# Dealing the spare slot tiles of a mixture-of-experts stage out to the experts in a fixed order, in a one-core hybrid attention / DeltaNet / MoE step

## The chip, the cores and the metric

One core of a Trainium2 chip runs the whole kernel. The metric is the device time of one execution in microseconds, lower is better. An execution is also profiled once, and its trace shows the span from its first instruction to its last.

## The reference, cut to what matters

The kernel computes one layer of a trunk for 256 context and 1024 latent tokens (1280 in all, model width 1024): a mixer (softmax attention beside a gated DeltaNet), then a hierarchical mixture of experts, then a final RMS norm. All of it is float32. The change touches the mixture of experts alone:

```python
g_top, g_idx = lax.top_k(gp, 1)                    # 1 of 4 groups
e_top, e_idx = lax.top_k(ep, TOP_K_IN_GROUP)       # 2 of the 4 experts in it
expert = g_idx * EXPERTS_PER_GROUP + e_idx         # 16 experts
hid = jax.nn.silu(einsum('td,edf->tef', t, w_gate)) * einsum('td,edf->tef', t, w_up)
hid = hid * combine[..., None]                     # 0 for the experts not chosen
y = einsum('tef,efd->td', hid, w_down)             # w_gate, w_up 1024x256, w_down 256x1024
```

## The kernel before

The kernel goes through seven stages, with a meeting of all five engines ("arrivals") between them. The sixth ends with the router and the expert tiles, the seventh combines.

**Slots and tiles.** Each token has two entries, one for each expert chosen: 2560 entries. They are sorted by expert into tiles of 128 slots, and a tile holds entries of one expert only. An expert with c entries needs ceil(c/128) tiles, and at least one is given to it. The number of tiles is fixed when the kernel is built, since no loop has a length read from data: MT = 2560/128 + 16 - 1 = 35, the most that any routing can need. For these inputs the reference's router gives the 16 experts 141, 53, 349, 403, 88, 66, 71, 107, 183, 152, 87, 164, 310, 136, 132 and 118 entries, which is 2, 1, 3, 4, 1, 1, 1, 1, 2, 2, 1, 2, 3, 2, 2 and 1 tiles, 29 together. Six tiles are spare.

**The table (VectorE, L1845 to L1899).** After the router's counts have been summed over the tokens on TensorE (L1062, L1064), VectorE works out `r_nt`, the tiles of each expert (L1846 to L1850), then `r_base`, the tiles of the experts ahead (L1853, L1855), then the running ends `r_nt + r_base` (L1857). Every one of these is a small instruction that waits for the one ahead of it. From the base it works out each entry's slot (L1859 to L1865) and one-hot matrices, with which TensorE (L1069) writes down the token of each slot. From the ends it counts for each tile the experts that have ended (L1882 to L1892): that is the tile's expert, held down to the last one by a minimum (L1886). The spare tiles lie behind all ends, so they run with expert 15 (weights of the ring slot that it is in); an empty slot holds token 0, and nobody reads what a spare tile puts out.

```python
v.tensor_scalar(r_nt, r_nt, 1.0, None, ALU.max)           # L1850
v.tensor_tensor(earlier, precedes, bc(r_nt...), ALU.mult) # L1853
v.tensor_reduce(r_base, earlier, AX.X, ALU.add)           # L1855
v.tensor_tensor(r_nt, r_nt, r_base, ALU.add)              # L1857
```

**The weights (SyncE's DMA queue, L632 to L657).** An expert's weights are 3 MB in three transfers (gate and up at L637, down at L639). They live in a ring of three places. The first three experts are loaded ahead of the stage. After that SyncE goes through the experts in order; `dn_mm` counts two halves of a down product for each tile:

```python
for e in range(NE):
    sp.wait_ge(S[f"ew_in{e % RING_E}"], landed(e, RING_E, 3))   # L652 expert e has landed
    sp.sem_inc(S["ew_ready"], 1)                                # L653 TensorE may use expert e
    if 1 <= e and e + RING_E - 1 < NE:
        through = sp.value_load(tab_i[... e - 1 ...])           # L655 2 x tiles up to expert e-1
        sp.wait_ge(S["dn_mm"], through)                         # L656
        expert_load(e + RING_E - 1)                             # L657 into the place of expert e-1
```

**The tiles (TensorE, L1099 to L1114).** In turn t TensorE does the gate and up products of tile t (16 matmuls, L1084), turns the hidden rows of tile t-1 (L1109), turns the slots of tile t+1 (L1079) and does the down product of tile t-1 (8 matmuls, L1094). Ahead of the gate and up products it waits until `ew_ready` has reached the tile's expert, plus one (L1103). GpSimd gathers the rows of each tile (L2060, an indirect DMA), ScalarE empties PSUM (L1370, L1389, L1379) and stores each tile (L1381), VectorE does the hidden product (L1906, L1908) and a copy (L1916).

**The last stage** gathers each token's two rows from the stored tiles by `pos_i` (GpSimd, L2071), combines, norms and stores them.

The small constants are one table of 485 columns, loaded once at the start, from which `small_row` takes rows (L137 to L140). `R`, the large buffer that holds the ring of weights and nearly all other tiles, is allocated behind it in SBUF.

Of the kernel before, what the change touches and what calls it, by code (L numbers as in the profile page):

```python
# [18 lines left out]
ALU = mybir.AluOpType  # L19
ACT = mybir.ActivationFunctionType  # L20
AX = mybir.AxisListType

P = 128
# [13 lines left out]
NE, FF = 16, 256  # L37
SLOTS = 128
MT = HT = 2 * T // SLOTS + NE - 1
# [33 lines left out]
def small_constants():  # L73

    step = [e % RING_E for e in range(NE)]
    rows = [np.arange(T // SLOTS) * float(SLOTS), np.arange(HT), (np.arange(NE)[None, :] < np.arange(NE)[:, None]).ravel(),
            [6144.0 * (step[e + 1] - step[e]) if e + 1 < NE else 0.0 for e in range(NE)], 128.0 * np.arange(MT + 1), np.arange(P) - 128.0, [4, 3, 2, 1]]
    row = np.concatenate([np.asarray(r, np.float32) for r in rows])
    return np.broadcast_to(row, (P, row.size)).copy()

# [11 lines left out]
def build(nc, a, outs):  # L92
    ctx = ExitStack()
    with ctx:
# [3 lines left out]
        def sem(name):  # L98
            return ctx.enter_context(nc.semaphore(name))


        const_np, small_np = shape_constants(), small_constants()
        cos_np, sin_np = rotary_tables()
        const_d = nc.inline_tensor(const_np, name="shape_constants")
# [29 lines left out]
        def small_row(n):  # L134
            sat[0] += n
            return small[:, sat[0] - n:sat[0]]

        filled, unit_no = small_row(T // SLOTS), small_row(HT)
        precedes = small_row(NE * NE).rearrange("p (e f) -> p e f", e=NE)
        slot_step, k128, lane, first4 = small_row(NE), small_row(MT + 1), small_row(P), small_row(4)  # L140


        prm = sb("prm", [P, P])
# [51 lines left out]
        S = {n: sem(n) for n in names}  # L195
# [3 lines left out]
        def count(name):  # L199


            counts[name] += 1
            return counts[name]
# [212 lines left out]
        def rsc(*shape):  # L416
            n = int(np.prod(shape))
            rat[0] += n
            r = R3[:, rat[0] - n:rat[0]]
            if len(shape) == 2:  # L420
                r = r.rearrange("p (a b) -> p a b", a=shape[0])
            return r
# [8 lines left out]
        r_cmp = rsc(HT * NE)  # L431
        r_nt, r_base = rsc(NE), rsc(NE)
# [235 lines left out]
        def _(pe):  # L668
# [179 lines left out]
            def values(i):  # L848
                _, nk, v0 = keys(QH[i][0])
                end = TURN0[i, 1] + len(slices(i))  # L850
                pe.wait_ge(S["pt_act"], emptied(end, "act"))
                if emptied(end, "dve") > 0:
                    pe.wait_ge(S["pt_dve"], emptied(end, "dve"))
                if i > 0:
                    pe.wait_ge(S["o_out"], i)
                for j in range(nk):
                    for g in range(2):
                        lo = slice(g * HD, (g + 1) * HD)
                        last = mm(ps[lo, 7, (i % 4) * P:(i % 4 + 1) * P], v_sb[:, v0 + j, lo], pT[i % 2][g][:, j, :],
                                  start=(j == 0), stop=(j == nk - 1))  # L860
                last.then_inc(S["pv_mm"], 1)
# [551 lines left out]
        def _(dve):  # L1413
            v = nc.vector

            def bc(x, shape):
                return x.to_broadcast([P] + shape)
# [431 lines left out]
            dve.wait_ge(S["dve_chain"], count("dve_chain"))  # L1849
            v.tensor_scalar(r_nt, r_nt, 1.0, None, ALU.max).then_inc(S["dve_chain"], 1)  # L1850
            dve.wait_ge(S["dve_chain"], count("dve_chain"))
            earlier = r_cmp[:, 0:NE * NE].rearrange("p (e k) -> p e k", e=NE)
            v.tensor_tensor(earlier, precedes, bc(r_nt.unsqueeze(1), [NE, NE]), ALU.mult).then_inc(S["dve_chain"], 1)  # L1853
            dve.wait_ge(S["dve_chain"], count("dve_chain"))
# [251 lines left out]
```

## Time and profile before

| | us |
|---|---|
| median of three runs | 2481.5 (2478.1 to 2483.27) |
| time of the profiled execution | 2483.28 |
| its span | 2481.4 |
| TensorE matmul busy | 2155.5 (87%) |
| VectorE / ScalarE / GpSimd busy | 943.3 / 673.1 / 217.0 |
| mean granted TensorE clock | 0.93 |

The profile has one line for each engine and kind of instruction. "Idle before" is time in which the engine stood still just ahead of an instruction, with what ended it. SPq is the queue of DMA issues and semaphore steps of SyncE. Times of a timeline are microseconds from the start of the span. A matmul of 128x512 in float32 goes through TensorE as several passes, and its row is that of the whole matmul.

### The profile page before, as it was taken

What the parts mean: (1) busy time and instruction counts of PE and PEld (TensorE: products, weight loads), DVE (VectorE), ACT (ScalarE), POOL (GpSimd) and SP (SyncE); (2) the same over time, 40 slices, a digit from 0 to 9 for tenths busy, and PEclk for the clock granted to TensorE, in tenths of its full rate; (3) what the DMA queues carried; (4) which work ended last, traced back from release to release, by engine and by line L of the source; (5) the groups of instructions that cost most, each with busy time, mean ns of one, the idle gap of its engine ahead of it and who ended that gap; (6) DMA issues with size and microseconds to landing.
All of it is one profiled execution on the core that took longest, in us unless ns stands there. A gap on an engine that the chain in (4) does not pass through costs nothing. (4 is left out here: it accounts for less than half of the span.)

```text
span 2481.4 us, 39269 instructions
## 1 busy us (share of the span) xinstructions
PE 2155.5 (87%) x16431; PEld 1329.5 (54%) x16431; DVE 943.3 (38%) x1820; ACT 673.1 (27%) x1366; POOL 217.0 (9%) x301
## 2 busy tenths in 40 slices
PE   5987999989998588987897999999998699899960
PEld 4545677665554487887754555555455444344420
DVE  3254666643784367667460011010233200000116
ACT  6122766652441223322230000000111122122223
POOL 2000000000000233232000000000000000000013
PEclk8997999999999799989998999999998699999985
DMA  9423000000100232332103121120413455765226
GB/s 325 142 87 114 11 4 1 2 38 25 36 1 0 44 64 44 64 62 42 55 0 94 27 50 26 26 68 1 146 66 128 137 183 182 259 236 207 85 102 203
DMA packets 256382, 210.09 MB, mean 85 GB/s; under 512 B 147468, under 2 KB 219472, under 8 KB 255568
## 3 DMA queue, kind: packets, MB, share of 16 engines
q1 hardware_dynamic: 242032, 158.16, 21.5%
q0 software_dynamic: 9136, 31.06, 3.9%
q10 hardware_dynamic: 5040, 18.35, 1.8%
q8 instruction: 133, 2.18, 0.4%
q14 instruction: 41, 0.34, 0.0%
HBM read 165.37 MB, written 42.01 MB: 84 GB/s over the span
## 5 line engine op out<-in xcount | busy, mean ns | idle before, releaser
L741 PE MATMUL ps<-R 128*128 128x512 f32 (+1 forms) x816 | 300.2, 529 | 11.3 <-SPq L529 8.4
L1008 PE MATMUL ps<-R 128*128 128x512 f32 (+1 forms) x768 | 286.3, 527 | 19.4 <-DMA R<-in_w_dn_br_dram 17.3
L1084 PE MATMUL ps<-R 128*128 x560 | 260.2, 620 | 25.4 <-SPq L653 22.2
L741 PEld LDWEIGHTS ps<-R 128*128 128x128 f32 x816 | 157.5, 194 | 151.0 <-issue 132.4
L1008 PEld LDWEIGHTS ps<-R 128*128 128x128 f32 x768 | 147.5, 193 | 151.7 <-issue 144.3
L900 PE MATMUL ps<-R 64*64 64x64 f32 x5120 | 179.3, 228 | 55.5 <-DVE R L1674 44.0
L900 PEld LDWEIGHTS ps<-R 64*64 64x64 f32 x5120 | 168.8, 143 | 73.0 <-DVE R L1674 47.3
L1084 PEld LDWEIGHTS ps<-R 128*128 128x128 f32 x560 | 111.0, 200 | 169.2 <-issue 169.2
L1749 DVE TENSOR_TENSOR R<-ps,R 128x512 f32<-128x512 f32 (+1 forms) x48 | 28.9, 602 | 393.9 <-ACT R L1341 393.1
L1916 DVE COPY R<-ps 128x256 f32<-128x256 f32 x35 | 14.9, 424 | 383.4 <-PE ps L1109 383.4
L1523 DVE TENSOR_SCALAR_CACHE_REDUCE R<-ps 128x512 f32<-128x512 f32 (+1 forms) x208 | 128.3, 666 | 60.6 <-PE ps L826 60.5
L1030 PE MATMUL ps<-R 128*128 128x512 f32 x320 | 142.4, 604 | 3.8 <-PEq L1017 3.8
L1010 PE MATMUL ps<-R 128*128 128x512 f32 (+1 forms) x384 | 145.4, 521 | 0.0
L1341 ACT ACTIVATE R<-ps 128x512 f32<-128x512 f32 (+1 forms) x48 | 25.2, 526 | 412.1 <-PE ps L1010 411.4
L2060 POOL DMA_INDIRECT R<-h_scratch,slot_i x35 | 32.9, 941 | 1125.0 <-DVE slot_i L1899 750.2
L1094 PE MATMUL ps<-R 128*128 x280 | 127.8, 599 | 1.5 <-DVE R L1916 1.3
L845 PEld LDWEIGHTS ps<-cst,R 128*128 128x128 f32 x800 | 87.7, 142 | 59.1 <-issue 48.6
L845 PE MATMUL ps<-cst,R 128*128 128x128 f32 x800 | 106.6, 282 | 5.7 <-ACT R L1239 2.9
L826 PE MATMUL ps<-R 64*128 64x512 f32 (+1 forms) x416 | 107.1, 619 | 3.7 <-SPq L513 3.6
L1229 ACT ACTIVATE R<-R 128x1536 f32<-128x1536 f32 (+1 forms) x80 | 108.6, 1357 | 3.0 <-DVE R L1532 2.9
L1010 PEld LDWEIGHTS ps<-R 128*128 128x128 f32 x384 | 73.1, 190 | 64.4 <-issue 61.2
L1030 PEld LDWEIGHTS ps<-R 128*128 128x128 f32 x320 | 61.3, 194 | 78.6 <-issue 73.9
(266 smaller groups left out, 2675.1 us busy)
## 6 DMA issues: line engine op xcount, KB each, us to landing
R<-in_w_mod_dram SPq DMA_DIRECT2D x12, 2048.0 KB, 9.0
slot_output<-R ACTq DMA_DIRECT2D x35, 512.0 KB, 3.5
R<-in_w_gate_e_dram SPq DMA_DIRECT2D x16, 1024.0 KB, 6.3
R<-in_w_up_e_dram SPq DMA_DIRECT2D x16, 1024.0 KB, 10.1
R<-in_w_down_e_dram SPq DMA_DIRECT2D x16, 1024.0 KB, 12.1
R<-in_w_in_dram SPq DMA_DIRECT2D x30, 512.0 KB, 5.4
R<-tu_scratch SPq DMA_DIRECT2D x80, 128.0 KB, 3.2
R<-in_x_sample_dram SPq DMA_DIRECT2D x16, 512.0 KB, 6.1
```

Of the source, the lines that this page charges most:

```text
L741: last = mm(ps[:, u % 4, 0:w], w_sb[n % NW][:, k, :], hT[:, k, c0:c0 + w], start=(k == 0), stop=(k == KD - 1))
L826: last = mm(ps[:, 2 * (u % 2) + g, 0:w], qT[lo, h4, qt * P:(qt + 1) * P], kT[lo, c0 + j * 512:c0 + j * 512 + w], start=True, stop=True)
L845: last = turn128(ps[:, 4 + v % 3, k * P:(k + 1) * P], s_sb[i % 2][g][:, j * 512 + k * P:j * 512 + (k + 1) * P], ident)
L900: last = mm(ps[lo, bank, a * C:(a + 1) * C], lhs(a)[lo], rhs(a)[lo], start=start and (alone or a == 0), stop=stop and (alone or a == PAIRS ...
L1008: mm(ps[:, o + x, 0:w], wk[:, x, k, :], hT[:, k, c0:c0 + w], start=(k == 0), stop=(k == KD - 1))
L1010: last = mm(ps[:, o + 2 + x, 0:w], wb[:, x, k, :], (aoT, odT)[x][:, k, c0:c0 + w], start=(k == 0), stop=(k == 3))
L1030: last = mm(ps[:, 2 * (n % 2) + h, :], mT[:, k, n * P:(n + 1) * P], ow[k][:, h * 512:(h + 1) * 512], start=(k == 0), stop=(k == KD - 1))
L1084: last = mm(ps[:, 2 + t % 2, :], hsT[t % 2][:, k, :], R[:, bass.ds(at + (RB + k * 512), 512)], start=(k == 0), stop=(k == KD - 1))
L1094: last = mm(ps[:, 5 + u % 3, :], hidT[t % 2][:, k, :], R[:, bass.ds(at + (RB + 4096 + k * D + h * 512), 512)], start=(k == 0), stop=(k == 1))
L1229: f(s_sb[i % 2][g][:, 0:w], s_sb[i % 2][g][:, 0:w], ACT.Exp, bias=shift[i % 2][g], accum_out=sums[qt % 2][:, g, h4:h4 + 1]).then_inc(S["p_ ...
L1523: v.tensor_scalar(s_sb[i % 2][g][:, j * 512:j * 512 + w], ps[:, 2 * (u % 2) + g, 0:w], HD ** -0.5, None, ALU.mult, ALU.max, accum_out=tops ...
L2060: pool.indirect_dma_start(hs[t % 2], None, h2_d, bass.IndirectOffsetOnAxis(ap=slot_i[:, t:t + 1], axis=0)).then_inc(S[f"hs_in{t % 2}"], 16)
```

## The change

Three small VectorE instructions are put between L1850 and L1853. They sum the tiles over the experts, compare "sum + place of the expert in the order" with 35, and give one more tile to each expert for which that is smaller. The place is the expert's number with its four bits reversed: 0, 8, 4, 12, 2, 10, 6, 14, 1, 9, 5, 13, 3, 11, 7, 15 is the order in which experts are served. These 16 numbers are a new row at the end of the small constants (501 columns in place of 485). Everything that is worked out from `r_nt` (bases, slots, each tile's expert, the counts on which the loads of weights wait) follows by itself. The number of tiles stays 35.

```diff
-            [... 128.0 * np.arange(MT + 1), np.arange(P) - 128.0, [4, 3, 2, 1]]
+            [... 128.0 * np.arange(MT + 1), np.arange(P) - 128.0, [4, 3, 2, 1],
+            [int(f"{e:04b}"[::-1], 2) for e in range(NE)]]
...
-        slot_step, k128, lane, first4 = small_row(NE), small_row(MT + 1), small_row(P), small_row(4)
+        slot_step, k128, lane, first4, turn_of = small_row(NE), small_row(MT + 1), small_row(P), small_row(4), small_row(NE)
...
             v.tensor_scalar(r_nt, r_nt, 1.0, None, ALU.max).then_inc(S["dve_chain"], 1)
             dve.wait_ge(S["dve_chain"], count("dve_chain"))
+            v.tensor_reduce(r_base[:, 0:1], r_nt, AX.X, ALU.add).then_inc(S["dve_chain"], 1)
+            dve.wait_ge(S["dve_chain"], count("dve_chain"))
+            v.tensor_scalar(r_cmp[:, 0:NE], turn_of, r_base[:, 0:1], float(MT), ALU.add, ALU.is_lt).then_inc(S["dve_chain"], 1)
+            dve.wait_ge(S["dve_chain"], count("dve_chain"))
+            v.tensor_tensor(r_nt, r_nt, r_cmp[:, 0:NE], ALU.add).then_inc(S["dve_chain"], 1)
+            dve.wait_ge(S["dve_chain"], count("dve_chain"))
             earlier = r_cmp[:, 0:NE * NE].rearrange("p (e k) -> p e k", e=NE)
```

## Rows read from the trace of the kernel before

**Rows 1.** The page: the span, and the chain that ended last, by engine

```profile
span 2481.4 us, 39269 instructions
...
PE 41%; DVE 2%; DMA 2%; SPq 1%; issue 1%; ACT 1%; POOL 0%; DVEq 0%; ACTq 0%; PEldq 0%; POOLq 0%
```

**Rows 2.** Waits of TensorE, 1940 to 2405 us: total us, times, longest

```profile
PE ps L1084 <- SPq L653: 22.2, 6, 5.9
PE ps L1079 <- DMA R<-h_scratch,slot_i: 5.6, 1, 5.6
```

**Rows 3.** Timeline of TensorE: start, us, line, count, [idle before <- releaser]

```profile
1981.21 7.03 PE L1084 MATMUL ps<-R 128*128 x16
...
1996.34 8.83 PE L1084 MATMUL ps<-R 128*128 x16 [3.51 <-SPq L653]
...
2086.18 3.64 PE L1094 MATMUL ps<-R 128*128 x8
2093.26 9.88 PE L1084 MATMUL ps<-R 128*128 x16 [3.43 <-SPq L653]
...
2113.59 9.96 PE L1084 MATMUL ps<-R 128*128 x16 [5.88 <-SPq L653]
...
2131.09 7.13 PE L1084 MATMUL ps<-R 128*128 x16 [2.97 <-SPq L653]
...
2146.02 8.83 PE L1084 MATMUL ps<-R 128*128 x16 [3.22 <-SPq L653]
...
2208.41 8.63 PE L1084 MATMUL ps<-R 128*128 x16 [3.23 <-SPq L653]
...
2244.68 7.03 PE L1084 MATMUL ps<-R 128*128 x16
...
2381.96 7.03 PE L1084 MATMUL ps<-R 128*128 x16
```

**Rows 4.** Timeline of SyncE's DMA issues, same columns

```profile
2089.86 0.37 SPq L637 DMA_DIRECT2D R<-in_w_gate_e_dram  x1
2090.26 0.58 SPq L637 DMA_DIRECT2D R<-in_w_up_e_dram  x1
2090.89 2.16 SPq L639 DMA_DIRECT2D R<-in_w_down_e_dram  x1
...
2108.78 4.61 SPq L639 DMA_DIRECT2D R<-in_w_down_e_dram  x1
2128.15 0.37 SPq L637 DMA_DIRECT2D R<-in_w_gate_e_dram  x1
...
2279.20 0.37 SPq L637 DMA_DIRECT2D R<-in_w_gate_e_dram  x1
```

**Rows 5.** Waits of SyncE's queue, 1700 to 2400 us: total us, times, longest

```profile
SPq L637 <- PE ps L1094: 280.3, 13, 43.5
```

**Rows 6.** Issues that read the down weights: time from issue to landing

```profile
DMA to landing us min/median/max: 11.4/12.1/13.8
```

**Rows 7.** Timeline of VectorE between the router's sums and the table

```profile
1929.25 0.32 DVE L1848 TENSOR_REDUCE R<-R 128x16 f32<-128x160 f32 x1
1929.61 0.17 DVE L1850 TENSOR_SCALAR R<-R 128x16 f32<-128x16 f32 x1
1929.81 0.42 DVE L1853 TENSOR_TENSOR R<-small,R 128x256 f32<-128x256 f32 x1
...
1930.73 0.17 DVE L1857 TENSOR_TENSOR R<-R 128x16 f32<-128x16 f32 x1
1930.93 0.18 DVE L1859 TENSOR_SCALAR R<-R 128x16 f32<-128x16 f32 x1
```

**Rows 8.** Windows: us, PE, PEld, DVE, ACT, POOL busy, PEclk, DMA share, GB/s

```profile
2094.00:2104.00 10.00, 10.00 (x26) 4.70 (x24) 0.55 (x2) 0.55 (x2) 0.00 (x0) 0.76 0.83 303
...
2155.00:2193.00 38.00, 38.00 (x118) 19.06 (x117) 4.71 (x12) 10.37 (x19) 3.74 (x4) 1.00 0.69 233
```

**Rows 9.** The row gathers of the tiles (L2060): time from issue to landing

```profile
DMA to landing us min/median/max: 4.0/4.4/7.6
```

More of the change, by code:

```diff
@@ L76, in small_constants @@
     rows = [np.arange(T // SLOTS) * float(SLOTS), np.arange(HT), (np.arange(NE)[None, :] < np.arange(NE)[:, None]).ravel(),
-            [6144.0 * (step[e + 1] - step[e]) if e + 1 < NE else 0.0 for e in range(NE)], 128.0 * np.arange(MT + 1), np.arange(P) - 128.0, [4, 3, 2, 1]]
+            [6144.0 * (step[e + 1] - step[e]) if e + 1 < NE else 0.0 for e in range(NE)], 128.0 * np.arange(MT + 1), np.arange(P) - 128.0, [4, 3, 2, 1],
+            [int(f"{e:04b}"[::-1], 2) for e in range(NE)]]
     row = np.concatenate([np.asarray(r, np.float32) for r in rows])
```

## The prediction

> **What bounds the kernel now.** I went from the page's chain of waits to the stage that the change touches. The chain is made of TensorE above all [rows 1], so time is won only where TensorE stands still or runs slowly. In the expert stage (1940 to 2405 us) the table of waits shows one costly wait: the gate and up products (L1084) stood still for SyncE's step at L653 six times, 22.2 us together; the other row is the start of the stage [rows 2]. The timeline shows which tiles these were. L1084 has one row per tile; counted from tile 0 they are tiles 3, 11, 12, 13, 14 and 19 [rows 3]. Against the tile counts 2, 1, 3, 4, 1, 1, 1, 1, 2, 2, 1, 2, ... these are the first tiles of experts 2, 5, 6, 7, 8 and 11: each follows an expert with one tile (1, 4, 5, 6, 7 and 10), and no other tile does. Expert 15 has one tile too, but nothing follows it.
>
> The code says why. The release of expert e+1 (L653) stands in SyncE's order behind the load of expert e+2, and that load waits for the last down product of expert e-1. TensorE does that product in the turn after, behind the first gate and up products of expert e. If expert e has one tile, the next thing that TensorE wants is expert e+1. So it ends the down product (2086.18 + 3.64 = 2089.82), only then does SyncE issue three transfers (2089.86 to 2093.05), and at 2093.26 TensorE goes on [rows 3, 4]. Expert e+1 itself has long been in SBUF: it is the issuing that is waited for. If expert e has two tiles or more, the issuing (3 us) lies beside 7.03 us of gate and up products.
>
> The tiles otherwise run at a fixed pace: from 2244.68 (tile 22) to 2381.96 (tile 34) are 12 turns of 11.44 us. From tile 2 (1981.21) to tile 34 are 400.75 us for 32 turns, so 400.75 - 32 x 11.44 = 34.7 us is lost in the stage [rows 3]. The parts: 22.2 us of idle time; slower gate and up products right after it, against 7.03 us: 1.80 + 2.85 + 2.93 + 0.10 + 1.80 + 1.60 = 11.1 us; and 1.4 us of small gaps (0.23 us a stop).
>
> **The change, part by part.** The sum of tiles is 29, so the experts with a place below 6 get one: 0, 8, 4, 12, 2 and 10. The counts become 3, 1, 4, 4, 2, 1, 1, 1, 3, 2, 2, 2, 4, 2, 2, 1, together 35. Experts 4 and 10 have lost their single tile; 1, 5, 6, 7 keep it.
>
> *Stops removed.* Those behind experts 4 and 10: 3.43 + 2.85 + 0.23 = 6.5 us and 3.23 + 1.60 + 0.23 = 5.1 us [rows 3], 11.6 us in all.
>
> *Stops kept.* Four, ahead of tiles 4, 15, 16 and 17. Before, they cost what the rows of tiles 3, 12, 13 and 14 show: 34.7 - 11.6 = 23.1 us. One is larger than the others: 5.88 us, because the issue of one transfer took 4.61 us, against 2.16 us for the same line one expert earlier [rows 3, 4]. I see nothing in the routing that causes it and count it as chance; then a stop is the mean of the other five: idle (3.51 + 3.43 + 2.97 + 3.22 + 3.23)/5 = 3.27, slow products (1.80 + 2.85 + 0.10 + 1.80 + 1.60)/5 = 1.63, gap 0.23, so 5.1 us, and four are 20.5 us. The stage's loss goes from 34.7 to 20.5: 14.2 us won. Bounds: if all four are like the cheapest row (2.97 + 0.10 + 0.23 = 3.3 us), 21.5 us are won; if the first is as tile 3's (5.5) and the other three like the dearest (5.88 + 2.93 + 0.23 = 9.0 us), 34.7 - 32.6 = 2.1 us.
>
> *The clock.* Windows behind a stop show a granted clock of 0.76 and windows of steady work 1.00: part of the stretch ran at 1.2 GHz, in place of 2.4 [rows 8]. Five of the six stops were followed by slower products, one (2.97 us idle) was not [rows 3]. The Trainium skill, TensorE: Matmul & The Clock Gate, Part 1, has it that "the default state is throttled, and activity releases the throttle". If by that rule every stop kept is paid with a slow stretch (the mean of the five is 2.2 us), the four cost 4 x (3.27 + 2.2 + 0.23) = 22.8 us and 11.9 us are won, in place of 14.2. I take the mean over all rows, as one in six got away, and keep the other value inside the range.
>
> *Instructions added.* Three of VectorE, on 16 columns or fewer. They lie on the path: router sums, table, L1069, slot numbers, first gather, first tile; TensorE waits for that gather [rows 2]. The nearest rows, on 128x16, start 0.20 us apart (L1850 to L1853, L1857 to L1859) [rows 7], so three cost 0.6 us. A scalar operand read from SBUF at this size has no row: at most it is like the reduction over 160 columns, 0.36 us from start to start, and then three cost 1.1 us; since each waits for the one ahead, it cannot be below 3 x 0.17 = 0.5 us. Sum row: 0.6 us lost.
>
> *Loads moved.* 13 loads of 3 MB wait on the new counts [rows 5]. A load is released at the last down product of expert e-1 and used by expert e+2: between lie all tiles of experts e and e+1, at least two. Landing takes some 12.1 us (at most 13.8) after its last transfer's issue, which is 1.0 us after the first [rows 4, 6], so about 15 us. The tightest place is two single experts in a row: from the load of expert 8 (2128.15) to its first tile (2146.02) are 18 us [rows 3, 4], 3 us to spare. Experts 5, 6 and 7 keep that pattern unchanged, so nothing new is late. The last load moves behind tile 29 (issued at 2279.20 before, about 2334 after) and is wanted at tile 34, about 2368. The 13 loads cover more of the stage instead of ending ahead of it; what they run beside is the gather of each tile (4.4 us, at most 7.6) [rows 9], which the code issues two turns ahead of its use, and the store of each tile, waited for two turns later. Cost nothing; without that cover, the excess over the slack.
>
> *Spare tiles moved.* Six tiles run earlier with another expert's weights: the same 35 gathers, products and stores, no cost. The last stage gathers the same rows from other places: nothing.
>
> *The table of constants.* 64 bytes more for each of 128 partitions, once, with the other constants at the start: nothing by bytes (8 KB). It moves `R` by 64 bytes, see the third rival.
>
> **The sum.** 14.2 - 0.6 = 13.6 us won. The profiled execution took 2483.3 us (span 2481.4), so it would take 2469.7; it lies 1.8 us above the median of the runs, by which the same gain gives 2467.9. I say 2469, between the two. A measurement of this kernel can tell about 0.2% (5 us) from no change.
>
> **Rivals.**
> 1. *The kept stops become dearer.* For: a 5.88 us stop exists in the before run, at the load of expert 7, which is again in the run of single experts; if it belongs to that load (its addresses or place), it stays, with its slow products: 5.88 - 3.27 = 2.6 and 2.93 - 1.63 = 1.3, so 3.9 us less won, 2473. If more than one stop is like it, 2.1 - 0.6 = 1.5 us are won and the time is 2480: no measurable change. Against: 12 of the 13 later loads were issued without such a delay. Chance: 0.2 for the first form, 0.08 for the second.
> 2. *The stops move instead of going.* If the stops came from late weights, and not from the issuing order, dealing tiles out would shift them to other experts: before minus nothing, plus 0.6 us, 2482. For: the releaser named is the step after a landing wait. Against: TensorE goes on 0.2 us after the last issue in both stops whose issues are shown (2093.05 to 2093.26, 2113.39 to 2113.59) [rows 3, 4], and each stop follows a single-tile expert. The same time would come out if the stage did not get the spare tiles as I count them. Chance 0.05.
> 3. *Slower: the 64 bytes.* `R` goes from a start that is a multiple of 128 bytes to one that is a multiple of 64 only, under all transfers. To end over 5 us slower, 13.6 + 5 = 19 us have to be lost where DMA is exposed. The chain holds 2% of DMA [rows 1], 50 us, so those transfers would have to become some 38% longer. No row shows that alignment matters; nearly all else is hidden. Chance 0.03, time 2487. The Trainium skill, DMA: Bandwidth & Descriptors, "How a descriptor splits into AXI transactions", says that a read that starts off a 256-byte boundary also fetches the bytes from the boundary on. By it a 4 KB row read out of `R` would fetch 192 bytes too much in place of 128, an estimate of 1.5% on stores that are hidden; no row here shows it.
>
> **How the numbers follow.** Four stops near the mean: 0.64, at 2469. Rival 1: 0.28, at 2473 or 2480. Rival 2: 0.05 at 2482. Rival 3: 0.03 at 2487. The forecast's own bounds are 21.5 - 0.6 = 20.9 us won, 2461 from the median, and on the other side rival 1's first form plus half of the spread between the three runs (2.6 us), 2476. That range leaves out the second form of rival 1, rivals 2 and 3, about 0.16. Faster by over 0.2% (below 2476.5): the forecast and the first form, 0.84. Within 0.2%: the second form and rival 2, 0.12. Slower 0.04.
>
> **What would show it.** TensorE's wait for L653: four times, about 13 us together, ahead of tiles 4, 15, 16 and 17, none elsewhere. Steady turns still 11.44 us. From tile 2 to tile 34 about 386.6 us, in place of 400.75. Loads of experts 7, 8 and 9 issued one turn apart, plus the stop, and the last load about 2334. Three VectorE rows of about 0.17 us ahead of the 128x256 product, and the first gather 0.6 us later relative to the router's sums. Everything outside the stage the same within 1 us. I am wrong if the stops number more than four, if a stop is ended by a landing, if the turns with a load beside them are longer than 11.44 us, or if stages ahead of the router change.

## The result and the profile after

The changed kernel takes 2464.56 us (median of four runs, 2463.08 to 2467.85) beside 2479.8 us of the kernel before (four runs): ratio 0.9939, 95% interval 0.9922 to 0.9956. Measured again later (number 8 below) it was 2466.39 beside 2476.84 us: ratio 0.996, 0.9945 to 0.9975. The two intervals share 0.9945 to 0.9956, about 11 to 14 us. The profiled execution took 2467.85 us. Two executions, one of run 1 (2747.1 us) and one of the kernel before beside runs 5 to 7 (3011.29 us), had a granted clock of 0.81 and 0.73 in place of 0.93 and are left out of the ratios, which also need not be exactly the quotients of the medians.

The wait table of TensorE, 1940 to 2405 us, stands against [rows 2] (the added lines of code move L1084 to L1086, L1094 to L1096, and in SyncE's queue L653 to L655, L637 to L639 and L639 to L641):

```profile
PE ps L1086 <- SPq L655: 12.6, 4, 3.6
```

Six stops have become four, and 22.2 us of waiting 12.6. The timeline of TensorE in the changed kernel, against [rows 3] (start, us, line, count, [idle before <- releaser]); the first row is tile 2, the last tile 34:

```profile
1978.73 7.03 PE L1086 MATMUL ps<-R 128*128 x16
...
2004.55 10.19 PE L1086 MATMUL ps<-R 128*128 x16 [2.76 <-SPq L655]
...
2137.32 8.66 PE L1086 MATMUL ps<-R 128*128 x16 [3.62 <-SPq L655]
...
2153.57 8.82 PE L1086 MATMUL ps<-R 128*128 x16 [3.01 <-SPq L655]
...
2170.17 8.83 PE L1086 MATMUL ps<-R 128*128 x16 [3.20 <-SPq L655]
...
2366.44 7.03 PE L1086 MATMUL ps<-R 128*128 x16
```

Counted from tile 0 the stops are ahead of tiles 4, 15, 16 and 17. From tile 2 to tile 34 are 387.71 us, 21.6 us above 32 turns of 11.44 us; before it was 400.75 and 34.7. The stage has won 13.0 us. The span is 15.5 us shorter, though: 2.5 us lie ahead of tile 2 (1981.21 to 1978.73), and behind tile 34 nothing changed (2481.4 - 2381.96 = 99.4 us, 2465.9 - 2366.44 = 99.5 us).

The three new instructions in VectorE's timeline, with the rows around them, against [rows 7]:

```profile
1926.73 0.18 DVE L1852 TENSOR_SCALAR R<-R 128x16 f32<-128x16 f32 x1
1926.94 0.17 DVE L1854 TENSOR_REDUCE R<-R 128x1 f32<-128x16 f32 x1
1927.14 0.24 DVE L1856 TENSOR_SCALAR R<-small,R 128x16 f32<-128x16 f32 x1
1927.42 0.18 DVE L1858 TENSOR_TENSOR R<-R 128x16 f32<-128x16 f32 x1
1927.63 0.43 DVE L1861 TENSOR_TENSOR R<-small,R 128x256 f32<-128x256 f32 x1
```

They take 1927.63 - 1926.94 = 0.69 us. L1856, which reads a scalar from SBUF and does two operations, takes 0.24 us; L1852, with one operation and a constant, 0.18. Which of the two differences costs the 0.06 us isn't shown. SyncE's queue, against [rows 4]: the down weights of experts 5 and 7.

```profile
2066.16 4.40 SPq L641 DMA_DIRECT2D R<-in_w_down_e_dram  x1
...
2134.77 2.34 SPq L641 DMA_DIRECT2D R<-in_w_down_e_dram  x1
```

The long issue is now that of expert 5's down weights (4.40 us) and no longer that of expert 7's (4.61 before, 2.34 now). It lies under expert 3's tiles, where TensorE does not wait for it. The last load is issued from 2332.31 on.

### The profile page after: what moved, and what is told of

Same layout as the page of the kernel before. It is cut to its first block and busy times, and to the rows that moved or that the text cites. A ratio compares the mean times of both kernels' runs of the same rounds, so it can differ in the third digit from the quotient of the medians.

```text
span 2465.9 us, 39272 instructions
## 1 busy us (share of the span) xinstructions
PE 2146.9 (87%) x16431; PEld 1324.6 (54%) x16431; DVE 943.7 (38%) x1823; ACT 673.5 (27%) x1366; POOL 216.9 (9%) x301
## 5 line engine op out<-in xcount | busy, mean ns | idle before, releaser
L1086 PE MATMUL ps<-R 128*128 x560 | 257.2, 614 | 15.8 <-SPq L655 12.6
L1086 PEld LDWEIGHTS ps<-R 128*128 128x128 f32 x560 | 109.8, 197 | 157.4 <-issue 157.4
L1924 DVE COPY R<-ps 128x256 f32<-128x256 f32 x35 | 14.9, 425 | 370.2 <-PE ps L1111 370.2
L1096 PE MATMUL ps<-R 128*128 x280 | 127.7, 599 | 1.3 <-DVE R L1924 1.3
```

Of the source, the lines that this page charges most:

```text
L1086: last = mm(ps[:, 2 + t % 2, :], hsT[t % 2][:, k, :], R[:, bass.ds(at + (RB + k * 512), 512)], start=(k == 0), stop=(k == KD - 1))
L1096: last = mm(ps[:, 5 + u % 3, :], hidT[t % 2][:, k, :], R[:, bass.ds(at + (RB + 4096 + k * D + h * 512), 512)], start=(k == 0), stop=(k == 1))
```

## The experiments

The diffs are cut: the semaphore step behind each VectorE instruction, the names of buffer slices and the middle of long lines (...) are left out.

**1. The layout alone.** The kernel before with 16 unused columns behind the small constants, so that `R` moves by 64 bytes.

```diff
-... np.arange(P) - 128.0, [4, 3, 2, 1]]
+... np.arange(P) - 128.0, [4, 3, 2, 1],
+            np.zeros(NE)]
```

> The kernel before with 16 unused columns added to the small constants: R moves by 64 bytes, nothing else changes. Theory (the gain is stops removed in the expert stage, the rest chance): same time as before within 2.5 us, six stops of TensorE for SyncE's release, 400 us plus or minus 4 from tile 2 to tile 34. Rival A (the move of R is what made the stages ahead of tile 2 some 2.5 us shorter in the changed kernel): 2 to 3 us faster than before, all of it ahead of tile 2. Rival B (the move costs): slower by 2 us or more.

Measured: 2482.07 against 2478.82 us, ratio 1.0007 (0.9996 to 1.0018). Six stops, 397.5 us from tile 2 to tile 34, tile 2 at 1983.4. The move of `R` neither gains nor costs anything that can be seen, and it does not bring tile 2 forward. It leaves no room for a loss above 0.2%.

**2. The instructions without the dealing.**

```diff
-v.tensor_scalar(r_cmp[:, 0:NE], turn_of, r_base[:, 0:1], float(MT), ALU.add, ALU.is_lt)
+v.tensor_scalar(r_cmp[:, 0:NE], turn_of, r_base[:, 0:1], 0.0, ALU.add, ALU.is_lt)
```

> The changed kernel with the threshold 35 made 0, so that the three VectorE instructions run and no expert gets a spare tile. Theory: the gain is gone, six stops ahead of tiles 3, 11, 12, 13, 14 and 19, tile 2 to tile 34 about 400 us, time of before plus 0.66 us. Rival A (part of the gain comes from the layout of the tables): 2 us faster than before at the same six stops.

Measured: 2477.3 against 2478.82 us, ratio 0.9997 (0.9986 to 1.0008). The gain is gone, and the six stops are back ahead of tiles 3, 11, 12, 13, 14 and 19. From tile 2 to tile 34 it took 396.7 us. Tile 2 began at 1978.5, as early as in the changed kernel's profile, in a kernel that is not faster. So the early start is no part of what the dealing does: over all eleven profiles it lies between 1976.7 and 1983.4 us. What sets it stays open. The three profiles without the new instructions start at 1980.5 to 1983.4, the eight with them at 1976.7 to 1981.4, and the interval of this run leaves room for the 2 us of its rival, so a small effect of the layout outside the stage is not ruled out. The time behind tile 34 lies between 98.4 and 101.2 us in the eleven.

**3. Spare tiles dealt out, but not to single experts.** The row `turn_of` gives the first six places to experts 0, 2, 3, 8, 9 and 11, which have two tiles or more.

```diff
-            [int(f"{e:04b}"[::-1], 2) for e in range(NE)]]
+            [0, 6, 1, 2, 7, 8, 9, 10, 3, 4, 11, 5, 12, 13, 14, 15]]
```

> Spare tiles dealt out too, but to experts that already have two tiles or more (0, 2, 3, 8, 9, 11), so that all six single experts with a successor stay single. Theory (a stop belongs to a single expert, whatever the spacing of the loads): six stops, each about 5 us, the stage loses 30 to 36 us and the time is that of before plus 0.7 us, within 3 us. Rival (what helps is that loads are spread over more of the stage): some 13 us faster than before, as the change.

Measured: 2475.85 against 2478.82 us, ratio 0.9995 (0.9983 to 1.0007). TensorE's wait table:

```profile
PE ps L1086 <- SPq L655: 19.6, 6, 3.8
```

The loads are as spread out as in the change, all 35 tiles belong to their experts, and nothing is won: 397.1 us from tile 2 to 34, 31.0 us lost in six stops. They stand ahead of tiles 4, 14, 15, 16, 17 and 24, which with these counts (3, 1, 4, 5, 1, 1, 1, 1, 3, 3, 1, 3, ...) are again the first tiles behind experts 1, 4, 5, 6, 7 and 10. This rules out that spreading the loads is what makes the gain.

**4. Spare tiles dealt to exactly the single experts.** Now experts 1, 4, 5, 6, 7 and 10 have the first six places.

```diff
-            [int(f"{e:04b}"[::-1], 2) for e in range(NE)]]
+            [6, 0, 7, 8, 1, 2, 3, 4, 9, 10, 5, 11, 12, 13, 14, 15]]
```

> The six spare tiles dealt to exactly the six experts with a single tile and a successor (1, 4, 5, 6, 7, 10). Theory: no stop of TensorE for SyncE's release, tile 2 to tile 34 about 366.5 us, 21 us less than the changed kernel's 387.7, time about 2444 us, 36 us less than before. Rival (with no slack lost to stops, loads of 3 MB every two turns are landed too late): stops stay, ended by landings, and the gain over the changed kernel is under 10 us.

Measured: 2448.3 against 2478.82 us, ratio 0.9874 (0.9858 to 0.989). The wait for the release is gone from TensorE's table, and the stage runs without a loss: tile 2 and tile 34 in its timeline are

```profile
1981.38 7.03 PE L1086 MATMUL ps<-R 128*128 x16
...
2347.46 7.03 PE L1086 MATMUL ps<-R 128*128 x16
```

366.08 us for 32 turns. Experts with two tiles each, eight in a row (4 to 11), leave a load of 3 MB time enough. The stage is as forecast, but the time is 4 us above what I had written. I had taken some 21 us, the loss in the change's first profile, off its first time, 2464.6 us; its second profile (number 8) loses only 15.9. Against the kernel before it fits: the profiles of runs 1 to 3, with six stops, lose 31 us, and 31 less 0.7 for the table is about the 30.5 us by which the medians differ.

**5. and 6. The release ahead of the wait.** With the counts of the kernel before (5) and of the change (6), SyncE announces expert e+1 before it waits for the place that expert e+2's load needs.

```diff
+sp.wait_ge(S["ew_in0"], landed(0, RING_E, 3))
+sp.sem_inc(S["ew_ready"], 1)
 for e in range(NE):
-    sp.wait_ge(S[f"ew_in{e % RING_E}"], landed(e, RING_E, 3))
-    sp.sem_inc(S["ew_ready"], 1)
+    if e + 1 < NE:
+        sp.wait_ge(S[f"ew_in{(e + 1) % RING_E}"], landed(e + 1, RING_E, 3))
+        sp.sem_inc(S["ew_ready"], 1)
     if 1 <= e and e + RING_E - 1 < NE:
```

> The kernel before with its tile counts, but SyncE releases expert e+1 ahead of the wait for the load of expert e+2, not behind it. Theory (the stops are SyncE's order, not landings): the stops ahead of tiles 3, 11 and 19 vanish. In the row of single experts 4 to 7 a load is now asked for only one turn (11.44 us) ahead of its use and lands about 13.4 us after its first issue, so stops of about 2 us, ended by a landing, stay ahead of tiles 12, 13 and 14. The stage loses 6 to 14 us in place of 34.7, time about 2455 us (2450 to 2460). Rival (weights are late anyway): six stops stay, under 8 us won.

> The changed kernel with the same earlier release. Theory: the stops ahead of tiles 4 and 15 vanish, two stops of about 2 us ended by landings stay ahead of tiles 16 and 17, the stage loses 4 to 9 us in place of 21.6, time about 2450 us (2446 to 2454). Rival: four stops stay, same time as the changed kernel.

Measured: (5) 2455.68 against 2477.71 us, ratio 0.9904 (0.9866 to 0.9942), 7.6 us lost in the stage in two stops, ahead of tiles 12 and 14, where three were expected. (6) 2451.2 us, ratio 0.9892 (0.9866 to 0.9918), 3.0 us lost in two stops, ahead of tiles 16 and 17. That is less than the 4 to 9 us expected: the second stop was only 0.68 us, and the products behind both ran at full pace (7.13 us). TensorE's waits in (5), then in (6):

```profile
PE ps L1087 <- SPq L656: 5.3, 2, 3.4
```

```profile
PE ps L1089 <- SPq L658: 2.5, 2, 1.8
```

What SyncE's own queue waits for in (5) shows what these stops are:

```profile
SPq L637 <- PE ps L1097: 138.8, 8, 43.4
SPq L656 <- DMA R<-in_w_down_e_dram: 130.2, 13, 11.8
```

The release (L656) now waits for landings. The load that ends the first stop, of expert 6, was asked for when tile 9 was done (SyncE's issues, and the row of tile 12 in TensorE's timeline):

```profile
2083.66 0.37 SPq L637 DMA_DIRECT2D R<-in_w_gate_e_dram  x1
...
2084.70 2.23 SPq L639 DMA_DIRECT2D R<-in_w_down_e_dram  x1
...
2098.51 8.58 PE L1087 MATMUL ps<-R 128*128 x16 [3.44 <-SPq L656]
```

It was wanted one turn later, at 2095.07 (2098.51 less the 3.44 us of idle time), and TensorE went on at 2098.51, 14.9 us after the first issue. In the kernel before this landing was not waited for. There the down weights of expert 6 were issued at 2090.89 and, by [rows 6], landed by 2104.7 at the latest, while TensorE came to tile 12 at 2107.71 (2113.59 less 5.88 [rows 3]): the stop ahead of tile 11, with the slow products behind it, had given the load its time. With SyncE's order mended that time is gone, and the landing becomes the thing waited for. The order explains most of the loss: 30.6 to 34.7 us with it (before, runs 1 and 2), 7.6 without, from the same tile counts.

**7. Dealing by count.** A version that does not lean on a list of experts: a spare tile goes to each expert with one tile, in order of number, while there are any.

```diff
-v.tensor_scalar(r_cmp[:, 0:NE], turn_of, r_base[:, 0:1], float(MT), ALU.add, ALU.is_lt)
-v.tensor_tensor(r_nt, r_nt, r_cmp[:, 0:NE], ALU.add)
+v.tensor_scalar(single, r_nt, 1.0, None, ALU.is_le)
+v.tensor_tensor(rk, precedes, bc(single.unsqueeze(1), [NE, NE]), ALU.mult)
+v.tensor_reduce(rank, rk, AX.X, ALU.add)
+v.tensor_scalar(given, rank, r_base[:, 0:1], float(MT), ALU.add, ALU.is_lt)
+v.tensor_tensor(given, given, single, ALU.mult)
+v.tensor_tensor(r_nt, r_nt, given, ALU.add)
```

> The spare tiles dealt by count and not by a fixed order: to the experts with one tile, in order of their numbers, as long as there are spare tiles. Six more VectorE instructions than the kernel before plus one sum, two of them on 256 columns (about 1.9 us in all by the rows of such instructions, against 0.7 us in the changed kernel). Theory: no stop, stage loss 0, 1.2 us above the run that deals to the singles by a fixed order: about 2447 us (2443 to 2451). Rival (later start of the stage costs more than its own length, through the clock): over 3 us above it.

Measured: 2446.48 against 2477.71 us, ratio 0.9874 (0.9845 to 0.9904); no stop, 366.09 us from tile 2 to tile 34. It is the fastest kernel here, with numbers 4 and 9 beside it, some 16 to 20 us ahead of the change. Its seven small instructions begin at 1924.98 and the next one at 1927.00, 2.0 us in all against 0.69; between 2446.5 and 2448.3 us that 1.3 us can't be seen.

**8. The change again, and 9. both remedies.** Number 9 is number 7 with the release of numbers 5 and 6 (the two diffs above together).

> The changed kernel once more, beside the kernel before on the same chip in five rounds. Theory (13 us of the stage less 0.7 us of table; the 2.5 us won ahead of tile 2 in the first profile were spread between executions): ratio 0.995 plus or minus 0.001, four stops, stage loss 19 to 23 us. Rival (part of the gain lies outside the stage): ratio 0.9935 or less.

> Dealing by count and the earlier release together. Theory: with no single expert left that has a successor there is no stop for the release to take away, so the time is that of the dealing by count alone, 2446 us within 3 us. Rival (the release also shortens something else): 3 us or more below it.

Measured: (8) 2466.39 us, ratio 0.996 (0.9945 to 0.9975), four stops at the same tiles, but 15.9 us lost in the stage and not 19 to 23. TensorE's rows of the four:

```profile
2004.91 8.70 PE L1086 MATMUL ps<-R 128*128 x16 [2.26 <-SPq L655]
...
2135.71 7.13 PE L1086 MATMUL ps<-R 128*128 x16 [3.13 <-SPq L655]
...
2150.30 8.82 PE L1086 MATMUL ps<-R 128*128 x16 [2.89 <-SPq L655]
...
2167.06 7.13 PE L1086 MATMUL ps<-R 128*128 x16 [3.36 <-SPq L655]
```

Two of them were followed by products at full pace, in the first profile none. So the same four stops cost 21.6 us once and 15.9 us another time. (9) 2446.65 us, ratio 0.9878 (0.9858 to 0.9897): where no single expert has a successor, the release has nothing to add.

## Why the prediction was right, point by point

**The bound.** Right, and shown from both sides. The loss of the stage by number of stops, in the profiles: six stops 34.7 (before), 31.4, 30.6 and 31.0 us (runs 1 to 3); four 21.6 and 15.9 us (change, run 8); none 0.0 us (runs 4, 7, 9). In every one of them the stops stand behind the single experts, wherever the dealing put these. Runs 5 and 6 show that SyncE's order makes most of the loss.

**Stops removed.** Experts 4 and 10 lost theirs, the only two. Their two rows had cost 11.6 us.

**Stops kept.** I had 20.5 us for four; the two profiles show 21.6 and 15.9. The price of 5.1 us a stop holds on the whole: the six profiles that have the old order (before, change, runs 1, 2, 3 and 8) lose 165.2 us in 32 stops, 5.2 each. It does not hold for one execution. No stop of the changed kernel is longer than 3.62 us, so rival 1 falls in both its forms. That the long issue was pure chance was too simple, though. In the change and in runs 3, 6 and 8, whose counts agree up to expert 2, the last one that this load waits for, the load of expert 5 has it every time (4.40, 4.40, 4.36, 4.45 us); with the counts of before that load never has it, and expert 7's has it in two of four profiles (4.61 us, and 3.68 in run 2 with a stop of 4.95 us; 2.00 in run 1, 1.99 in run 5). So the schedule has a part in it, and in the changed kernel it falls where TensorE doesn't wait. Against the mean stop of 3.27 us that was worth 2.6 us in the profile of before, 1.7 in run 2 and nothing in run 1. What I had read as the loss of the kernel before, 34.7 us, was itself a dear execution; the three other profiles with six stops lost 30.6 to 31.4 us. By them the change wins 31.0 - 18.8 = 12 us in the stage, with the mean of its two profiles, where I had 14.2.

**The clock.** The stretch behind a stop of the change (window, us, PE, PEld, DVE, ACT, POOL, PEclk, DMA share, GB/s), and steady work after it, against [rows 8]:

```profile
2137.00:2147.00 10.00, 9.68 (x27) 4.91 (x28) 0.70 (x2) 0.71 (x2) 0.00 (x0) 0.83 0.92 336
2183.00:2237.00 54.00, 54.00 (x163) 26.66 (x162) 5.30 (x14) 12.20 (x23) 3.75 (x4) 1.00 0.60 211
```

In the first profile of the change all four stops were paid with slow products (3.16 + 1.63 + 1.79 + 1.80 = 8.4 us over 7.03 each), and the stage lost 21.6 us, near the 22.8 us that I had for a slow stretch behind every stop. In run 8 two of four were (1.67 and 1.79 us over), and the mean over the rows was nearer. All 32 stops of the six profiles decide for the mean: 25 were followed by slow products and 7 were not, and the excess over 7.03 us is 1.62 us a stop, where the sum had 1.63 and the other reading 2.2. The Trainium skill, TensorE: Matmul & The Clock Gate, Part 1, has it that "activity releases the throttle"; the prediction had read this as a price paid at every stop, and the traces do not bear that out.

**Instructions added.** 0.6 us forecast, 0.69 measured. **Loads and spare tiles moved.** Nothing, as forecast: in runs 4, 7 and 9, with a load in nearly every second turn, all turns are still 11.44 us, and run 3 moves loads and tiles without an effect. The last load went out at 2332.3 (about 2334). The slack that I had read beside single experts was not there by itself, though: a load of expert e+2 goes out in the turn of expert e's first tile, so if both e and e+1 are single only one full turn lies between. The 18 us from expert 8's load to its first tile were one turn of 11.44 us and, for the rest, the two stops ahead of tiles 13 and 14 (2.97 and 3.22 us). Without the stops a turn is too short for a landing 12 to 15 us after the first issue [rows 4, 6], which is why runs 5 and 6 wait for it. In the change the stops stay there, and nothing came of it.

**The sum.** 13.6 us forecast; the stage's 12 us less 0.7 are 11.5 by the profiles. The profiled pair of executions differs by 15.4 us (2483.28 to 2467.85): 13.0 in the stage and 2.5 ahead of tile 2, the table's 0.69 us already taken off. The medians differ by 15.2 us, those of the second measurement by 10.5. The 2.5 us had no part in the sum. By its own signs the prediction was wrong there: it wanted everything outside the stage the same within 1 us, and VectorE began the table's work 2.9 us earlier (L1846 at 1928.89 before, L1848 at 1926.02 after). How much of either time is chance, the same pair of kernels shows: 15.2 us once and 10.5 us another time. Rival 2 falls by run 3 (the stops moved with the single experts and nothing was won, while the change did win), rival 3 by run 1, whose interval ends at 0.2% slower. In the chances the second form of rival 1 and rival 2 add up to 0.13 and not 0.12, and rival 3 alone is 0.03 and not 0.04.

**What the prediction left open** was the better question: of the six spare tiles only two went where a stop was. The same six tiles dealt to the single experts win 31 us, in place of some 13.

## What to carry to other kernels

When one queue both announces data that have long been there and waits for room for the next, look where the announcement stands: behind the wait, it makes the consumer wait for its own progress whenever a piece of work is as short as one turn. Count such pieces before dealing out padding, and give the padding to them; where it landed otherwise (run 3) it made no difference. Mend the order too, but expect the next reason (here the landing of the load, one turn after it was asked for) to stand right behind it.

## What the runs showed of the hardware

- The stop does not decide by its length whether slower products follow. Over the changed kernel, the kernel before and runs 1, 2, 3 and 8, idle times of 2.97, 3.27, 3.31, 2.78, 3.03, 3.13 and 3.36 us were followed by full pace (7.13 us), others of 2.26, 2.73 and 2.76 us by 8.70, 10.19 and 10.19 us. With the gap of 0.23 us one stop so costs from 3 to 7 us, up to 9 with a long issue, and the same kernel's stage differs by 5.7 us between executions.
- The issue of one 1 MB transfer of down weights holds SyncE's queue for 0.7 to 2.6 us in 129 of the 143 loads issued under the tiles of the eleven profiles, for 4.4 to 4.7 us in 12, and once each for 3.0 and 3.7. Which load it is goes partly with the schedule (see above); runs 4 and 7 have two and three of the long ones (one of run 4 from 2097.03, 4.49 us), all under running tiles and with no effect. What makes them long stays open.
